# Head norm of an mLSTM block: quotient folded into the norm, squares and gating moved to earlier units

## The chip, the cores and the metric

The kernel runs on one core of a Trainium2 chip. The metric is the time of one execution in microseconds of the device. A core has TensorE (PE; PEld is its weight load), VectorE (DVE), ScalarE (ACT), GpSimd (POOL) and the DMA queues, here above all SyncE's (SP). Each engine runs its own list of instructions in order and waits on semaphores.

## The reference, cut to what matters

The program is a decoder trunk of two layers on 256 tokens of width 1024 in float32. Only the end of the mLSTM mixer of layer 0 is touched. Per head (4 heads, value width 256) the reference computes

```
h = num / jnp.maximum(jnp.abs(den), jnp.exp(-m_t))[..., None]
...
h = h * lax.rsqrt(jnp.mean(h * h, axis=-1, keepdims=True) + EPS) * hnorm_g
h = h.astype(x.dtype) * jax.nn.sigmoid(o.reshape(Bsz, S, A_HEADS, A_V_DIM))
return h.reshape(Bsz, S, nv) @ w_out
```

`o` is a projection of the same normed input as q, k and v; `w_out` is the output projection, followed by the residual and a gated ConvFFN. With d = max(|den|, exp(-m_t)) the first two lines equal num / sqrt(mean(num^2) + EPS d^2), times the gain.

## The kernel before, in words

Every weight is cut into units of 1024 rows by 256 columns. Unit n lies in slot n % 3 of a ring: SP loads it into `raw` (`load`, L359; for n >= 3 it waits until the slot's low parts are done), ScalarE rounds it to a high part `whi` (`hi`, L505, which waits for the load and for TensorE's last use of the slot), and the low part `wlo = raw - whi` is computed in two halves (`lo`) by VectorE for slots 0 and 1 (L852) and by GpSimd for slot 2 (L464, four instructions). TensorE multiplies a unit as two column tiles (c 0 and 1), for each of 8 row blocks k with three matmuls (high by high, high by low, low by high): 48 matmuls (`unit`, L1319), the second half of the rows only when the second half of `wlo` is there. `part` runs some k only; with `k_wait` a unit goes k by k instead of tile by tile.

Units 0 to 11 are the input projection: 0 to 3 are q and k, 4 to 7 are v, 8 to 11 are o. Units 12 to 15 are the output projection (`U_AOUT` is 12), 16 onwards the first FFN. The order on each engine is written out by hand: each has a loop over u, and what lies between the units' own steps is placed by u and c. Behind unit u TensorE puts: u 5 the scores; u 6, 7 and 8 the denominators (matmuls with ones, into bank 7) and numerators (bank 3 + h) of heads 0 and 1, of head 2, of head 3; u 7 and u 9 the column sums of the squares `hsq` of heads 0 and 1 and of heads 2 and 3 (into banks 3 and 4).

VectorE reads each tile of a unit out of PSUM; ahead of the tile (u, c) it puts `head_done(h)` (L957: maximum with `EB`, reciprocal, product into `hm`) at (7,0), (7,1), (8,0), (9,0), and `head_normed(h)` (L971: reciprocal of `hroot`, product on `hm`) at (8,1), (9,1), (10,0), (10,1). At u 11, before the two tiles, `gated` (L897: `hm` times gain times sigmoid) and then `m_lo` (L905: the low part of the activation into `xsB`) run for k 0 to 3, and after the loop for 4 to 7. `lo(u + 2)` stands first in each u.

ScalarE has at u 7 to 9 `Abs` of the denominators and `Square` of `hm`; at u 8 and 10 the square root; `gate` (L550, the sigmoid of a tile) for k 0 to 3 at u 10; `m_hi` (L555) for k 0 to 3 at u 11, later ones and `hi(14)` after the loop. `hi(u + 3)` ends each u but the last.

TensorE's `outproj` (L1471) runs unit 12 for k 0 to 5 (`HEAD_K` is 6), waiting for `m_lo` of each k, then waits for VectorE's last tile, runs unit 13 for k 0 to 5, then k 6 and 7 of both, then units 14 and 15. The same function runs layer 1's output projection (`begun` is true there). VectorE's `outproj` (L1077) adds the residual and makes the FFN's input (`gained`, L880) and the sum of its squares; the FFN's norm and the first taps (`cb`, L1107 and L1111) follow.

Of the kernel before, what the change touches and what calls it, by code (L numbers as in the profile page):

```python
# [16 lines left out]
P = 128  # L17
D = 1024
S = 256
# [74 lines left out]
def build(nc, xT, vectors, b_if, a_w_in, a_w_out, w_kv, b_w_q, b_w_out, rel_bias, f_w_up,  # L94
          f_w_down, onehot, mask, group, out):
    ctx = ExitStack()
    with ctx:
# [115 lines left out]
        def sq(q):  # L213
# [40 lines left out]
        den_done, den_abs, dmax_done, dinv_done = (sem("den_done"), sem("den_abs"),  # L254
                                                   sem("dmax_done"), sem("dinv_done"))
        num_done, hm_done, hsq_done = sem("num_done"), sem("hm_done"), sem("hsq_done")
# [245 lines left out]
        def _(act):  # L502
# [96 lines left out]
            for u in range(12):  # L599
# [17 lines left out]
                if u == 5:  # L617

                    for b in range(2):
                        act.wait_ge(eb_done, b + 1)  # L620
                        a.activation(EB[:, 2 * b:2 * b + 2, :],
                                     bank[(3, 7)[b]][:, :].rearrange("p (h t) -> p h t", h=2),
                                     ACT.Copy).then_inc(eb_copied, 1)
                    for e in range(2 * AH):
# [4 lines left out]
                            .then_inc(dm_exp, 1)  # L629
                for h in {7: (0, 1), 8: (2,), 9: (3,)}.get(u, ()):  # L630

                    act.wait_ge(den_done, max(h + 1, 2))
                    a.activation(den[:, h, :], bank[7][:, (h % 2) * S:(h % 2 + 1) * S], ACT.Abs)\
                        .then_inc(den_abs, 1)
                    act.wait_ge(hm_done, h + 1)
                    a.activation(hsq[:, h, :, :], hm[:, h, :, :], ACT.Square).then_inc(hsq_done, 1)
                if u in (8, 10):
                    b = u // 10
                    act.wait_ge(hss_done, b + 1)
                    a.activation(hroot[:, 2 * b:2 * b + 2, :],  # L640
                                 bank[3 + b][:, :].rearrange("p (h t) -> p h t", h=2),
                                 ACT.Sqrt, bias=epsc[:, 0:1], scale=1.0 / DV)\
                        .then_inc(hroot_done, 1)
# [12 lines left out]
            for k in range(4, KD):  # L656
                m_hi(k)
            hi(14)

# [189 lines left out]
        def _(dve):  # L849
# [107 lines left out]
            def head_done(h):  # L957

                dve.wait_ge(den_abs, h + 1)
                v.tensor_tensor(den[:, h, :], den[:, h, :], EB[:, h, :], ALU.max)\  # L960
                    .then_inc(dmax_done, 1)
                dve.wait_ge(dmax_done, h + 1)
                v.reciprocal(den[:, h, :], den[:, h, :]).then_inc(dinv_done, 1)
                dve.wait_ge(dinv_done, h + 1)
                dve.wait_ge(num_done, h + 1)
                v.tensor_tensor(hm[:, h, :, :],
                                bank[3 + h][:, :].rearrange("p (c t) -> p c t", c=2),
                                den[:, h:h + 1, :].to_broadcast([P, 2, S]), ALU.mult)\
                    .then_inc(hm_done, 1)

            def head_normed(h):  # L971
# [4 lines left out]
                v.tensor_tensor(hm[:, h, :, :], hm[:, h, :, :],  # L976
# [3 lines left out]
            for u in range(12):  # L980
                lo(u + 2)
# [65 lines left out]
                if u == 11:  # L1047
                    for k in range(4):
                        gated(k)
                    for k in range(4):  # L1050
                        m_lo(k)
                for c in range(2):

                    if (u, c) in ((7, 0), (7, 1), (8, 0), (9, 0)):
                        head_done(((7, 0), (7, 1), (8, 0), (9, 0)).index((u, c)))
                    if (u, c) in ((8, 1), (9, 1), (10, 0), (10, 1)):
# [652 lines left out]
```

## Time and profile before

| | |
|---|---|
| median of 3 runs | 792.14 us (792.02 to 792.15) |
| the profiled execution | 791.78 us, its span 789.7 us |
| busy share PE / DVE / ACT / POOL | 97% / 68% / 58% / 29% |
| mean granted clock | 0.993 |
| the part touched | about 62 to 118 us of the span |

A row of a timeline gives start, duration, engine, line, operation and tiles; xN merges N instructions, and the brackets show the idle time before it and who ended it. Successive instructions of an engine overlap a little in the records, so a step is read as the distance of two starts. The PSUM tensor of banks 3 to 5 and that of 6 and 7 are both shown as `banks`.

### The profile page before, as it was taken

How to read it: one execution, taken by the hardware profiler on the slowest of the kernel's cores; microseconds unless marked ns; L12 is line 12 of the kernel's file. 1: busy time of each engine (PE TensorE's matmuls, PEld its weight loads, DVE VectorE, ACT ScalarE, POOL GpSimd, SP SyncE). 2: the span in 40 equal slices, each digit the busy share in tenths (PEclk: the TensorE clock that was granted, in tenths of full speed). 3: DMA queues.
4: the chain of work that ended last, by engine and by line, in shares of the span. 5: the costliest groups of instructions: out<-in, count | busy, mean ns of one | idle time of the engine just before them, and what ended most of it. 6: DMA issues, size and time to landing. Idle time of an engine off the chain costs nothing.

```text
span 789.7 us, 17137 instructions
## 1 busy us (share of the span) xinstructions
PE 765.8 (97%) x6534; PEld 751.4 (95%) x6534; DVE 535.2 (68%) x983; ACT 458.6 (58%) x608; POOL 226.7 (29%) x190
## 2 busy tenths in 40 slices
PE   8999989999999999999999999999999999999995
PEld 8989889999999999999999999999998999999995
DVE  5776867888878744646646646565678888788442
ACT  6552546756566546447647746835856665665451
POOL 2520222523422342222222220311232234222331
PEclk9999999999999999999999999999999999999998
DMA  9653426565555566754473374474426655554721
GB/s 293 203 165 107 135 82 212 174 200 190 182 182 184 186 193 205 226 191 141 131 236 128 104 246 149 149 230 139 152 83 201 226 186 187 183 189 147 238 93 53
DMA packets 139804, 136.23 MB, mean 173 GB/s; under 512 B 3585, under 2 KB 139089, under 8 KB 139764
## 3 DMA queue, kind: packets, MB, share of 16 engines
q1 hardware_dynamic: 127968, 130.11, 50.9%
q10 hardware_dynamic: 11796, 5.56, 2.8%
q8 instruction: 27, 0.44, 0.2%
q14 instruction: 13, 0.11, 0.1%
HBM read 134.54 MB, written 1.13 MB: 172 GB/s over the span
## 4 chain that ended last, share of the span: by engine, by line
PE 57%; DVE 22%; issue 10%; ACT 7%; DVEq 1%; DMA 1%; ACTq 0%; POOL 0%; POOLq 0%
DVE wlo L860 8%; PE bank L1315 7%; PE bank L1317 7%; PE bank L1316 7%; PE banks L1315 6%; PE banks L1317 6%; PE banks L1316 6%; PE bank L1539 3%; DVE cb L1107 3%; PE bank L1541 3%; PE bank L1540 3%; PE banks L1601 2%; ACT cb L690 2%; DVE bank L1101 2%; PE banks L1573 2%
## 5 line engine op out<-in xcount | busy, mean ns | idle before, releaser
L471 POOL TENSOR_TENSOR wlo<-raw,whi 128x512 fp32r<-128x512 f32 (+1 forms) x169 | 218.1, 1322 | 526.5 <-ACT whi L512 526.5
L512 ACT ACTIVATE whi<-raw 128x2048 fp32r<-128x2048 f32 (+1 forms) x136 | 238.1, 1751 | 199.2 <-PE bank L1317 106.1
L860 DVE TENSOR_TENSOR wlo<-raw,whi 128x1024 fp32r<-128x1024 f32 x161 | 197.1, 1262 | 15.0 <-ACT whi L512 14.3
L1315 PE MATMUL bank<-xsA,whi 128*128 128x256 f32 x568 | 159.4, 281 | 2.9 <-DVE wlo L937 1.9
L1317 PE MATMUL bank<-xsA,wlo 128*128 128x256 f32 x568 | 157.7, 278 | 0.0
L1316 PE MATMUL bank<-xsA,whi 128*128 128x256 f32 x568 | 157.6, 278 | 0.0
L1315 PE MATMUL bank<-xsB,whi 128*128 128x256 f32 x480 | 134.0, 279 | 0.4 <-DVE cb L1111 0.3
L1317 PE MATMUL bank<-xsB,wlo 128*128 128x256 f32 x480 | 132.6, 276 | 0.0
L1316 PE MATMUL bank<-xsB,whi 128*128 128x256 f32 x480 | 132.6, 276 | 0.0
L1315 PEld LDWEIGHTS bank<-xsA,whi 128*128 128x128 f32 x568 | 107.5, 189 | 4.7 <-issue 3.7
L1316 PEld LDWEIGHTS bank<-xsA,whi 128*128 128x128 f32 x568 | 107.5, 189 | 0.1
L1317 PEld LDWEIGHTS bank<-xsA,wlo 128*128 128x128 f32 x568 | 107.4, 189 | 0.0
L1315 PE MATMUL banks<-hs,whi 128*128 128x256 f32 x352 | 97.2, 276 | 0.0
L1316 PE MATMUL banks<-hs,whi 128*128 128x256 f32 x352 | 97.2, 276 | 0.0
L1317 PE MATMUL banks<-hs,wlo 128*128 128x256 f32 x352 | 97.2, 276 | 0.0
L1315 PEld LDWEIGHTS bank<-xsB,whi 128*128 128x128 f32 x480 | 90.1, 188 | 1.4 <-DVE cb L1111 0.5
L1316 PEld LDWEIGHTS bank<-xsB,whi 128*128 128x128 f32 x480 | 90.2, 188 | 0.0
L1317 PEld LDWEIGHTS bank<-xsB,wlo 128*128 128x128 f32 x480 | 90.1, 188 | 0.0
L1315 PEld LDWEIGHTS banks<-hs,whi 128*128 128x128 f32 x352 | 66.1, 188 | 0.0
L1317 PEld LDWEIGHTS banks<-hs,wlo 128*128 128x128 f32 x352 | 66.1, 188 | 0.0
L1316 PEld LDWEIGHTS banks<-hs,whi 128*128 128x128 f32 x352 | 66.1, 188 | 0.0
L1539 PE MATMUL bank<-whi,xsA 128*128 128x256 f32 x192 | 56.7, 296 | 0.0
(200 smaller groups left out, 1572.3 us busy)
## 6 DMA issues: line engine op xcount, KB each, us to landing
raw<-in_f_w_up SPq DMA_DIRECT2D x44, 1024.0 KB, 5.1
raw<-in_w_kv SPq DMA_DIRECT2D x24, 1024.0 KB, 5.3
raw<-in_f_w_down SPq DMA_DIRECT2D x16, 1024.0 KB, 5.1
raw<-in_b_w_q SPq DMA_DIRECT2D x12, 1024.0 KB, 5.3
raw<-in_a_w_in SPq DMA_DIRECT2D x10, 1024.0 KB, 5.8
raw<-in_f_w_down SPq DMA_DIRECT2D x8, 768.0 KB, 4.9
Bi<-bias_by_distance ACTq DMA_DIRECT2D x16, 320.0 KB, 4.6
raw<-in_a_w_out SPq DMA_DIRECT2D x4, 1024.0 KB, 5.2
```

The source lines that it names most:

```text
L471: o = g.tensor_tensor(wlo[s][:, ka:kb, :], raw[s][:, ka * CW:kb * CW] .rearrange("p (k c) -> p k c", c=CW), whi[s][:, ka:kb, :].bitcast(F3 ...
L512: o = a.activation(whi[s][:, k0:k1, :], raw[s][:, k0 * CW:k1 * CW] .rearrange("p (k c) -> p k c", c=CW), ACT.Copy)
L690: a.activation(cb[:, j, :], bank[FB[j]][:, 0:S], ACT.Identity, scale=conv_col(layer, 2, ch), bias=conv_col(layer, 3, ch))\
L860: v.tensor_tensor(wlo[s][:, ka:kb, :], raw[s][:, ka * CW:kb * CW].rearrange("p (k c) -> p k c", c=CW), whi[s][:, ka:kb, :].bitcast(F32), A ...
L1101: v.tensor_tensor(u, u, rstd[:, 0:S], ALU.mult).then_inc(ev_done, 1)
L1107: v.scalar_tensor_tensor(cb[:, j, 1:S], bank[FB[j]][:, 0:S - 1], conv_col(layer, 1, p * 2 + (KF * g + c)), cb[:, j, 1:S], ALU.mult, ALU.ad ...
L1315: t_.matmul(ps, hi_w, hi_x, start=first, stop=False)
L1316: t_.matmul(ps, hi_w, lo_x, start=False, stop=False)
L1317: return t_.matmul(ps, lo_w, hi_x, start=False, stop=last)
L1539: t_.matmul(ps, xs[:, k, 0, cs], whi[s][:, k, :], start=first, stop=False)
L1540: t_.matmul(ps, xs[:, k, 0, cs], wlo[s][:, k, :], start=False, stop=False)
L1541: mm = t_.matmul(ps, xs[:, k, 1, cs], whi[s][:, k, :], start=False, stop=last)
```

## The change

The denominators and `exp(-m)` are squared as they leave PSUM (`EB`, `den`), their maximum is taken for two heads at once (`den_bounded`), and `Square` reads the numerators from PSUM. `squares_joined` forms sum/(DV EPS) + d^2 for two heads; the root with scale EPS gives `hroot`, and `head_normed` multiplies the numerator in PSUM by its reciprocal. `head_done` and its reciprocals are gone.

On TensorE all four denominators follow unit 6 (banks 7 and 6). The squares of heads 0 and 1 are summed behind unit 7, those of heads 2 and 3 between k 3 and k 4 of unit 9, which now runs k 0 to 3 of both tiles first. Layer 0's output projection is cut at k 4 in place of 6. `gate` for k 0 to 3 moves to u 9 on ScalarE (before `hi(12)`), `m_hi` for them to u 10 (before `hi(13)`), `hi(14)` ahead of `m_hi(6)`. On VectorE `gated` 0 to 3 moves to (10,0), `lo(12)` to (11,0), and `lo(13)` behind the loop, one half after `gated` 4 and 5, the other after `gated` 6 and 7.

```diff
@@ ScalarE
-                                     ACT.Copy).then_inc(eb_copied, 1)
+                                     ACT.Square).then_inc(eb_copied, 1)
...
+                if u == 7:
+                    for b in range(2):
+                        act.wait_ge(den_done, 2 * b + 2)
+                        a.activation(den[:, 2 * b:2 * b + 2, :],
+                                     bank[7 - b][:, :].rearrange("p (h t) -> p h t", h=2),
+                                     ACT.Square).then_inc(den_sq, 1)
                 for h in {7: (0, 1), 8: (2,), 9: (3,)}.get(u, ()):
-                    act.wait_ge(den_done, max(h + 1, 2))
-                    a.activation(den[:, h, :], bank[7][:, (h % 2) * S:(h % 2 + 1) * S], ACT.Abs)\
-                        .then_inc(den_abs, 1)
-                    act.wait_ge(hm_done, h + 1)
-                    a.activation(hsq[:, h, :, :], hm[:, h, :, :], ACT.Square).then_inc(hsq_done, 1)
-                if u in (8, 10):
...
+                    act.wait_ge(num_done, h + 1)
+                    a.activation(hsq[:, h, :, :],
+                                 bank[3 + h][:, :].rearrange("p (c t) -> p c t", c=2), ACT.Square)\
+                        .then_inc(hsq_done, 1)
+                if u in (8, 9):
+                    b = u - 8
+                    act.wait_ge(hsum_done, 2 * b + 2)
+                    a.activation(hroot[:, 2 * b:2 * b + 2, :], hroot[:, 2 * b:2 * b + 2, :],
+                                 ACT.Sqrt, scale=EPS).then_inc(hroot_done, 1)
+                if u == 9:
+                    for k in range(4):
+                        gate(k)
                 if u == 10:
                     for k in range(4):
-                        gate(k)
+                        m_hi(k)
                 if u == 11:
                     for k in (4, 5):
                         gate(k)
-                    for k in range(4):
-                        m_hi(k)
                 else:
                     hi(u + 3)
             for k in (6, 7):
                 gate(k)
-            for k in range(4, KD):
+            for k in (4, 5):
                 m_hi(k)
             hi(14)
+            for k in (6, 7):
+                m_hi(k)
@@ VectorE
+            def den_bounded(b):
+                dve.wait_ge(den_sq, b + 1)
+                v.tensor_tensor(den[:, pair(b), :], den[:, pair(b), :], EB[:, pair(b), :], ALU.max)\
+                    .then_inc(dmax_done, 1)
+            def squares_joined(b):
+                dve.wait_ge(dmax_done, b + 1)
+                dve.wait_ge(hss_done, b + 1)
+                v.scalar_tensor_tensor(hroot[:, pair(b), :],
+                                       bank[7][:, :].rearrange("p (h t) -> p h t", h=2),
+                                       1.0 / (DV * EPS), den[:, pair(b), :], ALU.mult, ALU.add)\
+                    .then_inc(hsum_done, 2)
             def head_normed(h):
...
-                v.tensor_tensor(hm[:, h, :, :], hm[:, h, :, :],
+                v.tensor_tensor(hm[:, h, :, :],
+                                bank[3 + h][:, :].rearrange("p (c t) -> p c t", c=2),
                                 hrs[:, h:h + 1, :].to_broadcast([P, 2, S]), ALU.mult)\
                     .then_inc(hn_done, 1)
             for u in range(12):
-                lo(u + 2)
+                if u < 10:
+                    lo(u + 2)
...
+                    if (u, c) in ((7, 1), (9, 0)):
+                        den_bounded((u - 7) // 2)
+                    if (u, c) in ((8, 0), (9, 1)):
+                        squares_joined(u - 8)
+                    if (u, c) in ((8, 1), (9, 0), (10, 0), (10, 1)):
+                        head_normed(((8, 1), (9, 0), (10, 0), (10, 1)).index((u, c)))
+                    if (u, c) == (10, 0):
+                        for k in range(4):
+                            gated(k)
+                    if (u, c) == (11, 0):
+                        lo(U_AOUT)
+                        for k in range(4):
+                            m_lo(k)
...
             for k in (4, 6):
                 gated(k)
                 gated(k + 1)
+                lo(U_AOUT + 1, k0=KD // 2 * (k // 6), k1=KD // 2 * (k // 6 + 1))
                 m_lo(k)
                 m_lo(k + 1)
@@ TensorE
+                if u == 9:
+                    unit(U_IN + 9, xsA, [in_bank(18), in_bank(19)], wait_bank=waits, part=(0, 4))
+                    pe.wait_ge(hsum_done, 2)
+                    squares(1)
...
+                for h in range(AH) if u == 6 else ():
+                    pe.wait_ge(sd_done, h + 1 if h < 2 else AH)
+                    ps = bank[7 - h // 2][:, (h % 2) * S:(h % 2 + 1) * S]
...
+                if u == 7:
+                    pe.wait_ge(den_sq, 1)
+                    squares(0)
...
-                unit(u0 + 1, xs, banks[1], part=(0, HEAD_K))
-                unit(u0, xs, banks[0], k_wait=k_wait, part=(HEAD_K, KD))
-                unit(u0 + 1, xs, banks[1], part=(HEAD_K, KD))
+                unit(u0 + 1, xs, banks[1], part=(0, k0))
+                unit(u0, xs, banks[0], k_wait=k_wait, part=(k0, KD))
+                unit(u0 + 1, xs, banks[1], part=(k0, KD))
```

Here `k0` is 6 when `begun`, else 4; `squares(b)` waits for `hsq_done` of each head and sums the squares of two heads into bank 7.

## Rows read from the trace of the kernel before

**Rows 1.** The page: busy time of TensorE; a kind of weight load, KB, us to landing.

```profile
PE 765.8 (97%) x6534; PEld 751.4 (95%) x6534; DVE 535.2 (68%) x983; ACT 458.6 (58%) x608; POOL 226.7 (29%) x190
...
raw<-in_f_w_up SPq DMA_DIRECT2D x44, 1024.0 KB, 5.1
```

**Rows 2.** TensorE's waits, whole span: us in total, times, longest.

```profile
PE banks L1315 <- DVE cb L1111: 3.2, 7, 1.3
PE banks L1315 <- DVE xsB L908: 2.3, 1, 2.3
...
PE banks L1466 <- ACT hsq L636: 1.7, 1, 1.7
...
PE bank L1315 <- DVE X L927: 0.7, 1, 0.7
```

**Rows 3.** Timeline of TensorE: starts of units 9, 10, 12, 14, squares, end of 11.

```profile
82.83 0.36 PE L1315 MATMUL bank<-xsA,whi 128*128 128x256 f32 x1
...
88.40 0.59 PE L1466 MATMUL banks<-hsq,ones 128*128 128x256 f32 x2
...
91.08 0.70 PE L1466 MATMUL banks<-hsq,ones 128*128 128x256 f32 x2 [1.66 <-ACT hsq L636]
...
91.86 0.47 PE L1315 MATMUL bank<-xsA,whi 128*128 128x256 f32 x1
...
102.84 0.28 PE L1317 MATMUL bank<-xsA,wlo 128*128 128x256 f32 x1
105.47 0.36 PE L1315 MATMUL banks<-xsB,whi 128*128 128x256 f32 x1 [2.35 <-DVE xsB L908]
...
118.07 0.28 PE L1315 MATMUL bank<-xsB,whi 128*128 128x256 f32 x1
```

**Rows 4.** A window behind unit 12's start: busy by engine, clock, DMA share, GB/s.

```profile
106.10:109.40 3.30, 3.30 (x17) 3.30 (x17) 3.21 (x9) 1.82 (x5) 0.00 (x0) 0.50 0.56 194
```

**Rows 5.** A group of VectorE, 60 to 111: count, busy us, mean ns, idle before.

```profile
L963 DVE RECIPROCAL den<-den 128x256 f32<-128x256 f32 x4 | 7.0, 1753 | 0.1
```

**Rows 6.** Timeline of VectorE, 98 to 106.

```profile
98.33 1.74 DVE L974 RECIPROCAL hrs<-hroot 128x256 f32<-128x256 f32 x1
100.11 0.69 DVE L976 TENSOR_TENSOR hm<-hm,hrs 128x512 f32<-128x512 f32 x1
100.72 0.42 DVE L1069 TENSOR_TENSOR sig<-bank,rstd 128x256 f32<-128x256 f32 x1
101.05 2.35 DVE L860 TENSOR_TENSOR wlo<-raw,whi 128x1024 fp32r<-128x1024 f32 x2
103.32 1.67 DVE L902 SCALAR_TENSOR_TENSOR hm<-hm,vcols,sig 128x256 f32<-128x256 f32 x4
104.90 1.43 DVE L908 TENSOR_TENSOR xsB<-hm,xsB 128x256 fp32r<-128x256 f32 x4
```

**Rows 7.** Timeline of ScalarE, 92 to 97.

```profile
92.74 0.67 ACT L640 ACTIVATE hroot<-banks,epsc 128x512 f32<-128x512 f32 x1
93.43 1.28 ACT L553 ACT_TABLE_LOAD   x1
94.72 1.34 ACT L553 ACTIVATE sig<-sig 128x256 f32<-128x256 f32 x4
```

**Rows 8.** VectorE's and GpSimd's `lo` side by side, layer 1; GpSimd's alone.

```profile
588.38 3.56 DVE L860 TENSOR_TENSOR wlo<-raw,whi 128x1024 fp32r<-128x1024 f32 x2
...
584.43 6.42 POOL L471 TENSOR_TENSOR wlo<-raw,whi 128x512 fp32r<-128x512 f32 x4 [23.41 <-ACT whi L512]
...
111.82 5.04 POOL L471 TENSOR_TENSOR wlo<-raw,whi 128x512 fp32r<-128x512 f32 x4 [20.36 <-ACT whi L512]
```

**Rows 9.** ScalarE at layer 0's FFN norm; VectorE's last residuals in layer 1.

```profile
136.01 1.90 ACT L512 ACTIVATE whi<-raw 128x2048 fp32r<-128x2048 f32 x1
137.81 0.45 ACT L547 ACTIVATE rstd<-banks,epsc 128x256 f32<-128x256 f32 x1
...
597.70 0.73 DVE L927 TENSOR_TENSOR X<-X,bank 128x256 f32<-128x256 f32 x2
```

More of the change, by code:

```diff
@@ L1046, in _ @@
                             .then_inc(sd_done, 1)
[L1047 to L1051, printed above, removed]
-                for c in range(2):
-                    if (u, c) in ((7, 0), (7, 1), (8, 0), (9, 0)):
-                        head_done(((7, 0), (7, 1), (8, 0), (9, 0)).index((u, c)))
-                    if (u, c) in ((8, 1), (9, 1), (10, 0), (10, 1)):
-                        head_normed(((8, 1), (9, 1), (10, 0), (10, 1)).index((u, c)))
+                for c in range(2):
+                    if (u, c) in ((7, 1), (9, 0)):
[11 more added lines that the diff above has]
+                            m_lo(k)
                     t = 2 * u + c
@@ L1377, in first_wait, with squares @@
                     pe.wait_ge(lo_done[0], 2)
+            def squares(b):
+                for h in (2 * b, 2 * b + 1):
+                    pe.wait_ge(hsq_done, h + 1)
+                    ps = bank[7][:, (h % 2) * S:(h % 2 + 1) * S]
+                    t_.matmul(ps, ones[:], hsq[:, h, 0, :], start=True, stop=False)
+                    mm = t_.matmul(ps, ones[:], hsq[:, h, 1, :], start=False, stop=True)
+                mm.then_inc(hss_done, 1)
             pe.wait_ge(consts, 2)
@@ L1453, in _ @@
                     pe.wait_ge(ev_done, 2 * (4 + h) + 2)
+                    if h == 3:
+                        pe.wait_ge(den_sq, 2)
                     for c in range(2):
@@ L1460, in _ @@
                     mm.then_inc(num_done, 1)
-                if u in (7, 9):
-                    for h in (0, 1) if u == 7 else (2, 3):
-                        pe.wait_ge(hsq_done, h + 1)
-                        ps = bank[3 + h // 2][:, (h % 2) * S:(h % 2 + 1) * S]
-                        t_.matmul(ps, ones[:], hsq[:, h, 0, :], start=True, stop=False)
-                        mm = t_.matmul(ps, ones[:], hsq[:, h, 1, :], start=False, stop=True)
-                        if h % 2:
-                            mm.then_inc(hss_done, 1)
+                if u == 7:
+                    pe.wait_ge(den_sq, 1)
+                    squares(0)
             def outproj(u0, e0, xs, k_wait, q0, banks, begun):
+                k0 = HEAD_K if begun else KD // 2
                 if not begun:
-                    unit(u0, xs, banks[0], k_wait=k_wait, part=(0, HEAD_K))
+                    unit(u0, xs, banks[0], k_wait=k_wait, part=(0, k0))
                 pe.wait_ge(ev_done, e0)
```

32 lines of the change are left out of this document (6 added, 26 removed).

## The prediction, made before the changed kernel ran

> **What bounds the kernel now.** I read the page first: TensorE is busy 97% of the span [rows 1], so only time in which it waits, or runs slowly, is to be had. Then its waits over the whole span [rows 2]: the largest single ones are 2.3 us on `xsB` (L908) and 1.7 us on `hsq` (L636), both inside the change, and 1.3 and 0.7 us on `cb` and `X`, just behind it. The timeline of TensorE places them [rows 3]. Unit 9 begins at 82.83, the squares of heads 2 and 3 at 88.40; head 3's pair runs from 91.08 to 91.86 (0.8 a head), so it was due at 89.2 and is 1.8 late. Units 10 and 11 end with the matmul of 102.84. Unit 12 begins at 105.47 instead of 102.95: 2.5 lost. Unit 14, behind the change, begins at 118.07. A window shows one loss more [rows 4]: from 106.1 to 109.4, behind that idle time, the granted clock is 0.50 (1.2 GHz, not 2.4), and 3.3 us at half rate lose 1.65. From unit 9 to unit 14, then, 1.8 + 2.5 + 1.65 = 5.95 us are lost. The cause is VectorE, which from 95 to 106 goes from one instruction to the next [rows 6] while ScalarE waits for it.
>
> **The change, part by part.** (1) The quotient goes. VectorE loses four reciprocals of 1.75 us (7.0) [rows 5], and four products of `hm` like the one at 100.11 (0.69 each, 2.8) [rows 6]; four maxima of 128x256 become two of 128x512, by the rows of these two sizes (0.42 and 0.69) 0.3 less in all. It gains two `squares_joined` of 128x512 from PSUM. The trace has no such form; bounds are 0.42 (a 128x256 read of PSUM, row 100.72) and 1.75 (a reciprocal); I take 0.7, the 128x512 row at 100.11. Net about 8.7 us less on VectorE (7.0 + 2.8 + 0.3 - 1.4). ScalarE trades four `Abs` for two `Square` of twice the width: nothing. More important: `hsq` no longer waits for VectorE. ScalarE can square head 3 as soon as its numerator is in PSUM and `hi(11)` is through, about 84.2.
>
> (2) TensorE's work does not change in amount. The denominators of heads 2 and 3 move from behind units 7 and 8 into the group behind unit 6, so unit 8 begins 0.7 later and unit 9 at the same 82.83. Half of unit 9 (24 matmuls, 2.85) ends at 85.7; squares until 87.2, with no wait since 84.2 is before 85.7; unit 10 begins near 90.1 (before 91.86). The split restarts the pipeline once more, 0.2. At (102.84 - 91.86) for 95 matmuls, unit 11 ends at 101.2.
>
> (3) The new VectorE chain. Steps are distances of starts in [rows 6]: a product 0.61, a tile read 0.33, a `lo` of two 2.27 (half 1.13), four `gated` 1.58 (0.395 each), four `m_lo` 1.35 (0.34 each); a reciprocal and its hand-over 1.78. Reading (9,0) now comes at three quarters of unit 9, 89.0. Then `squares_joined(1)` 89.3 to 90.0; `hroot` on ScalarE 0.67 [rows 7], 90.8; `head_normed(2)` to 93.2; `gated` 0 to 3 to 94.8 (their sigmoids: table load 1.28 and 0.33 each [rows 7], first at 92.4, last at 93.4, never late); tile, `head_normed(3)`, tile: 97.8; `lo(12)` to 100.1; `m_lo` 0 to 3 from 100.1 to 101.5, the first before unit 11 ends. So unit 12 starts without a wait at 101.2, and with no idle time ahead of it I expect clock 1.00. Its first half lasts to 104.0. VectorE meanwhile: two tiles 102.1, `gated` 4 and 5 102.9, first half of `lo(13)` 104.1. New wait: 0.2. `m_lo` 4, 5 to 104.7, `gated` 6, 7 to 105.5.
>
> The Trainium skill (ScalarE: Activation LUTs, What ACT_TABLE_LOAD costs) gives a table load 1.28 us plus a drain of 1.38. The row agrees on the load and not on the drain: the sigmoid starts at 94.72, 0.01 after the load of 93.43 ends [rows 7]. By the page the first `gated` would come 0.6 later and the gain be 0.6 less; the measurement decides.
>
> (4) What is late next. `hi(14)` now stands before `m_hi(6)`, at about 103.4 to 105.3 (before 109.84), so GpSimd's `lo(14)` starts at 105.3, beside VectorE's `gated(7)`, `lo(13)` second half, `m_lo(6)` and `m_lo(7)`. Such a meeting shows in [rows 8]: two halves of `lo` that take 2.35 alone took 3.56, and GpSimd's four took 6.42 (5.04 in other places, 1.26 each): they alternate, and a VectorE instruction with two SBUF inputs waits for a whole GpSimd one, 1.2. With three such waits: `lo(13)` ends 107.9, `m_lo(6)` 109.4, `m_lo(7)` 111.0. TensorE ends the first half of unit 13 at 107.0 and wants k 6 at 108.4: waits of 1.1 and 0.8. The bounds are 0 (VectorE wins each time) and 3.0 (another turn lost). The Trainium skill (SBUF — State Buffer, Who interferes with whom) says the one that issues first gets the shared ports for the whole instruction, which would make the order at 105.3 decide; with VectorE first at each turn the sum would lose nothing here.
>
> Sum to unit 14: 5.95 - 0.2 (split) - 0.2 - 1.9 = 3.65; it begins at 114.4.
>
> (5) Behind it. SP's loads of 15 and 16 are issued when `lo(12)` and `lo(13)` are done, 100.1 and 107.9, that is 4.5 later than now, and land 5.1 later [rows 1], 105.2 and 113.0. ScalarE wants them at about 111.9 and 115.1: hidden, by 2 at the least. The load of 17 is earlier. Unit 12 now ends 2.8 before unit 14 begins (1.4 before), so `hi(15)`, the residuals, `lo(15)` and `lo(16)` are about 1.5 earlier against TensorE, and two `gained` no longer meet GpSimd. The 0.7 wait for `X` [rows 2] and its restart go: 0.9. The next is the root of the FFN norm: it runs at 137.81, held by a weight copy of 1.9 before it [rows 9], though the sums were issued near 136.0, so it is 1.4 late. In layer 1 the same holds (597.70 [rows 9]: the last residuals wait there for a `lo` on VectorE); in layer 0 that `lo` is GpSimd's, so they can move up. I expect the root 1.2 earlier against TensorE and `lo(19)` clear of GpSimd, and the waits for `cb` (1.3 and a short one, with restarts 1.8) to shrink by 1.6. From there each pair is TensorE's. Total 3.65 + 0.9 + 1.6 = 6.2. The profiled execution took 791.78 (span 789.7 and 2.1 around it) and would take 785.6; the median of the runs, 792.14, is 0.36 above it: **785.9**.
>
> **The rivals.** *VectorE is not held by GpSimd*: the 1.9 does not arise, gain 8.1, 784.0. For it: the semaphores may fall so that `lo(13)` is issued before GpSimd's first; against it [rows 8]. *The gain behind unit 14 is not had*: 3.65 alone, 788.5. For it: layer 1 has no wait for `X` and still waits on `cb`; against it the place of that `lo`. *The wait moves into unit 9 or 10*: if `squares_joined`, `hroot` and `gated` come 1 later than worked out, unit 12's first half pays it: gain 5.2, 786.9. *Slower*: the waits of 0.2, 1.1 and 0.8 come within 10 us, and the clock falls as it did at 106.1 [rows 4] but stays at 0.50 for the rest of the output projection. From the first fall at 108 to the end near 125, 17 us of which half is loss: 8.5 against the 6.2, 794.4. It decides from about 12 us at half clock. For it: the clock did fall here; against it: it fell behind 2.4 idle us and not behind the 1.7 at 91 or the 1.3 in the FFN [rows 2]. *The change does not do what it says*: the mean square of the unnormed numerator plus EPS times the squared denominator is the same norm, and no step waits for its own result, so I give it nothing.
>
> **Chances.** Forecast 50%, no hold 17%, nothing behind 15%, chain late 12%, slower 4%, 2% between. Something under 0.2% (1.6 us, about what can't be told from no change) needs most of the forecast to fail. Range 783.8 to 788.6: the first and second rival lie just inside. Faster 0.94, same 0.02, slower 0.04.
>
> **What would show it.** In the profile after: `hsq` reads a bank and TensorE has no wait for it; unit 12 at about 101 without a wait and clock 1.00 through 100 to 125; waits of TensorE on `xsB` L908's counterpart of about 2 us in sum, with VectorE's `lo(13)` and `m_lo` longer than 1.22 and 0.42; unit 14 near 114.4; no wait for `X`; the wait of 1.3 for `cb` nearly gone. The prediction is wrong if TensorE waits in unit 9, if the clock falls, or if what is gained at unit 14 is not at least kept at the end.

## The result, and the profile after

The changed kernel takes 783.12 us (782.97 to 783.64, 4 runs) and the kernel before 792.14 on the same chip; the ratio of the two is 0.989, 95% interval 0.9876 to 0.9905. The prediction was 785.9 with a range of 783.8 to 788.6: the sign was right, the gain was 9.0 us and not 6.2, and the time lies 0.7 below the range. The profiled execution has a span of 781.1 us, 8.6 less than before.

TensorE's waits over the whole span, in the profile after (us in total, times, longest); the rows for `hsq`, `xsB` and `X` of [rows 2] are gone, and one wait for `wlo` is new:

```profile
PE banks L1332 <- DVE cb L1128: 2.2, 7, 1.2
...
PE bank L1332 <- DVE wlo L865: 0.3, 1, 0.3
```

The timeline of TensorE in the profile after answers to [rows 3]: start of unit 9, squares of heads 2 and 3 in its middle, start of unit 12, of unit 13 with its wait, of unit 14, of unit 16 (first FFN unit):

```profile
83.22 0.36 PE L1332 MATMUL bank<-xsA,whi 128*128 128x256 f32 x1
...
86.07 0.38 PE L1403 MATMUL banks<-hsq,ones 128*128 128x256 f32 x1
...
101.42 0.28 PE L1332 MATMUL banks<-xsB,whi 128*128 128x256 f32 x1
...
104.56 0.35 PE L1332 MATMUL bank<-xsB,whi 128*128 128x256 f32 x1 [0.26 <-DVE wlo L865]
...
112.81 0.28 PE L1332 MATMUL bank<-xsB,whi 128*128 128x256 f32 x1
...
123.69 0.28 PE L1332 MATMUL bank<-xsA,whi 128*128 128x256 f32 x1
```

Unit 9 begins 0.39 us later than before. That comes from the prologue, where nothing was edited, so I count from unit 9. Unit 14 comes 29.59 us behind it (35.24 before): 5.65 gained, where 3.65 was forecast. Unit 16 comes 40.47 behind it; it began at 129.81 before, 46.98 behind: 6.5 gained in all. Unit 19, the second unit of the FFN's second pair, begins at 140.88, and at 149.40 before: 8.9 gained. From there on the two traces run alike, and less the 0.39 this is the 8.6 of the spans to 0.1.

The windows after (columns as in [rows 4]) have the clock at 1.00 from unit 12 on, where the kernel before had 0.50:

```profile
101.40:104.40 3.00, 2.90 (x26) 2.70 (x24) 3.00 (x8) 2.21 (x5) 0.00 (x0) 1.00 0.88 294
104.40:110.00 5.60, 5.44 (x48) 5.47 (x49) 3.56 (x9) 1.93 (x3) 4.39 (x2) 1.00 0.39 124
```

VectorE's timeline after, where [rows 6] had its packed stretch; the chain is the one that the prediction wrote down, and ends 0.3 us behind it (the prologue's 0.39):

```profile
89.72 0.68 DVE L976 SCALAR_TENSOR_TENSOR hroot<-banks,den 128x512 f32<-128x512 f32 x1
...
91.10 1.75 DVE L984 RECIPROCAL hrs<-hroot 128x256 f32<-128x256 f32 x1
92.89 0.69 DVE L986 TENSOR_TENSOR hm<-banks,hrs 128x512 f32<-128x512 f32 x1
93.50 1.66 DVE L907 SCALAR_TENSOR_TENSOR hm<-hm,vcols,sig 128x256 f32<-128x256 f32 x4
...
98.13 2.35 DVE L865 TENSOR_TENSOR wlo<-raw,whi 128x1024 fp32r<-128x1024 f32 x2
100.40 1.42 DVE L913 TENSOR_TENSOR xsB<-hm,xsB 128x256 fp32r<-128x256 f32 x4
```

What was misjudged shows where GpSimd's `lo(14)` meets VectorE. First VectorE, then GpSimd, each instruction by itself:

```profile
105.40 0.48 DVE L907 SCALAR_TENSOR_TENSOR hm<-hm,vcols,sig 128x256 f32<-128x256 f32 x1
105.80 1.22 DVE L865 TENSOR_TENSOR wlo<-raw,whi 128x1024 fp32r<-128x1024 f32 x1
106.93 0.42 DVE L913 TENSOR_TENSOR xsB<-hm,xsB 128x256 fp32r<-128x256 f32 x1
107.27 0.42 DVE L913 TENSOR_TENSOR xsB<-hm,xsB 128x256 fp32r<-128x256 f32 x1
...
105.61 3.23 POOL L470 TENSOR_TENSOR wlo<-raw,whi 128x512 fp32r<-128x512 f32 x1 [16.36 <-ACT whi L511]
108.80 1.29 POOL L470 TENSOR_TENSOR wlo<-raw,whi 128x512 fp32r<-128x512 f32 x1
```

VectorE's four instructions keep their lengths. GpSimd's first one takes 3.23 us, not 1.29: it waits until VectorE's last `m_lo` ends at 107.69. The prediction had it the other way round.

### The profile page after: what moved, and what is told of

The parts are those of the page before. It is cut to its first block, busy times and chain, and to the rows that moved or that the text cites. A ratio compares the mean times of both kernels' runs of the same rounds, so it can differ in the third digit from the quotient of the medians.

```text
span 781.1 us, 17126 instructions
## 1 busy us (share of the span) xinstructions
PE 762.8 (98%) x6534; PEld 749.3 (96%) x6534; DVE 525.0 (67%) x975; ACT 457.9 (59%) x606; POOL 226.9 (29%) x190
## 4 chain that ended last, share of the span: by engine, by line
PE 62%; DVE 19%; issue 10%; ACT 5%; DMA 1%; DVEq 1%; ACTq 0%; POOL 0%; POOLq 0%
PE bank L1332 8%; PE bank L1333 8%; PE bank L1334 8%; DVE wlo L865 6%; PE banks L1332 6%; PE banks L1333 6%; PE banks L1334 6%; DVE cb L1124 3%; PE bank L1564 3%; PE bank L1566 3%; PE bank L1565 3%; PE banks L1626 2%; DVE bank L1118 2%; ACT cb L695 2%; PE banks L1598 2%
```

## The experiments

Medians of 4 to 12 runs. A ratio is a kernel's time to that of the kernel before, run beside it. "Against 783.1" means the changed kernel, which ran again (`after_again`) on the chip of `e_mid`, `e_cut6` and `e_gate11`; the other kernels ran on other chips, so differences of less than 1 us from it are not told apart there by the times alone. Gains and losses at a unit are counted from the start of unit 9.

> The changed kernel once more, beside its variants on the same chip. All theories: 783.1 us, 9.0 under the kernel before.

Measured 783.05 (782.83 to 783.61), ratio 0.9899 (0.9881 to 0.9916).

**GpSimd let in 2 us earlier.** `hi(14)` ahead of the gates of k 6 and 7 (`e_pool`):

```diff
                 if u == 11:
                     for k in (4, 5):
                         gate(k)
-                else:
-                    hi(u + 3)
+                hi(u + 3)
             for k in (6, 7):
                 gate(k)
-            for k in (4, 5):
-                m_hi(k)
-            hi(14)
-            for k in (6, 7):
+            for k in (4, 5, 6, 7):
                 m_hi(k)
```

> The changed kernel with hi(14) ahead of the gates of k 6 and 7, so that GpSimd's lo(14) asks for the ports at about 103.5, 2 us earlier, while VectorE is in the first half of lo(13), and VectorE then has a gap before m_lo(4). Theory A, that GpSimd gets in only where VectorE leaves a gap between instructions with two SBUF inputs: here it gets in, m_lo 4 to 7 and lo(13) wait one to three GpSimd instructions, and TensorE waits 1 to 2.5 us: 784.1 to 785.6. Theory B, that VectorE always wins: 783.1 to 783.4.

Measured 786.93, ratio 0.9947 (0.993 to 0.9964): 3.9 against 783.1, more than either theory had. VectorE's instructions from 104 on, then GpSimd's first ones, in the trace of this kernel:

```profile
104.20 1.28 DVE L909 TENSOR_TENSOR xsB<-hm,xsB 128x256 fp32r<-128x256 f32 x1
105.41 1.51 DVE L909 TENSOR_TENSOR xsB<-hm,xsB 128x256 fp32r<-128x256 f32 x1
106.84 1.51 DVE L903 SCALAR_TENSOR_TENSOR hm<-hm,vcols,sig 128x256 f32<-128x256 f32 x1
108.28 1.49 DVE L903 SCALAR_TENSOR_TENSOR hm<-hm,vcols,sig 128x256 f32<-128x256 f32 x1
...
103.33 1.88 POOL L470 TENSOR_TENSOR wlo<-raw,whi 128x512 fp32r<-128x512 f32 x1 [14.43 <-ACT whi L511]
105.16 1.48 POOL L470 TENSOR_TENSOR wlo<-raw,whi 128x512 fp32r<-128x512 f32 x1
```

VectorE's first half of `lo(13)` ends at 104.07 and `m_lo(4)` starts at 104.20. There GpSimd, which has asked since 103.33, gets in, and from then on each VectorE instruction waits for one of GpSimd's: four that take 0.42 or 0.48 alone take 1.28 to 1.51, 4.0 us more in sum. TensorE then waits for `m_lo(6)`, which stands behind these four and the second half of `lo(13)` and comes at 110.8:

```profile
PE banks L1328 <- DVE xsB L909: 2.7, 1, 2.7
```

and behind this idle time the granted clock is 0.50 again (from 112.5 to 115.7; the matmuls come 0.21 apart). Theory B falls: VectorE is held by GpSimd, and here that costs 3.9 us, about 1.6 of them by the half clock, where in the changed kernel the same meeting 2 us later costs nothing. Two things differ, the instant of the request and the pause of 0.13 us; the runs below take them apart.

**The opposite.** `hi(14)` behind `m_hi` 6 and 7 (`hi14_last`):

```diff
-            for k in (4, 5):
-                m_hi(k)
-            hi(14)
-            for k in (6, 7):
+            for k in range(4, KD):
                 m_hi(k)
+            hi(14)
```

> The changed kernel with hi(14) behind m_hi 6 and 7 again, so that GpSimd's lo(14) asks for the ports at about 106.5. Theory A, from the trace of the changed kernel, that the meeting at 105.6 costs VectorE nothing: 783.1. Theory of the prediction, that it costs 1 to 2 us wherever it happens: it is shorter here, 782 to 782.7.

Measured 784.33 (783.46 to 784.34), ratio 0.9909 (0.9892 to 0.9927), against 783.1: slower by 1.2 in the medians, which neither theory had; but two of the five runs, at 783.46 and 783.65, lie where the changed kernel's upper ones do, and the two intervals overlap. GpSimd asks at 108.19, behind VectorE's last `m_lo` (107.66), so there is no meeting at all, and at unit 14 it is where the changed kernel is: the meeting at 105.6 was indeed free. The loss lies behind (1.0 us by unit 19 in this trace, of a run at 784.33): `lo(14)` ends at 113.2 instead of 112.6, SP's load of unit 17 waits for it, ScalarE waits for that load (its `hi(17)`: first the changed kernel's, then this one's), and `lo(17)` meets one `gained` more:

```profile
118.79 1.92 ACT L511 ACTIVATE whi<-raw 128x2048 fp32r<-128x2048 f32 x1 [1.92 <-DMA raw<-in_f_w_up]
```

```profile
119.88 1.92 ACT L511 ACTIVATE whi<-raw 128x2048 fp32r<-128x2048 f32 x1 [3.05 <-DMA raw<-in_f_w_up]
...
122.30 1.16 DVE L883 SCALAR_TENSOR_TENSOR xsA<-X,vcols,xsA 128x256 fp32r<-128x256 f32 x1 [0.40 <-ACT xsA L522]
...
PE banks L1330 <- DVE cb L1126: 1.1, 1, 1.1
```

**The last wait taken away.** First half of `lo(13)` ahead of `gated` 4 and 5 (`e_lo13`):

```diff
             for k in (4, 6):
+                if k == 4:
+                    lo(U_AOUT + 1, k1=KD // 2)
                 gated(k)
                 gated(k + 1)
-                lo(U_AOUT + 1, k0=KD // 2 * (k // 6), k1=KD // 2 * (k // 6 + 1))
+                if k == 6:
+                    lo(U_AOUT + 1, k0=KD // 2)
```

> The changed kernel with the first half of lo(13) ahead of gated 4 and 5 instead of behind them. Theory: TensorE's last wait here (0.3 us, restart 0.2, at 104.56) goes and nothing else is late: 782.6 to 782.8. Rival, that VectorE then leaves a gap before m_lo(4) or lets GpSimd in at 105.6: 783.5 to 785.

Measured 784.84 (784.72 to 785.24), ratio 0.9921 (0.9906 to 0.9936), against 783.1. The rival holds. The wait before unit 13 is gone, but the last `m_lo` pair now meets GpSimd, 2.93 us where it took 0.76, and TensorE waits 0.8 for it in two pieces and, behind unit 18, 1.0 more for `cb`. At unit 14 the loss is 0.86, at unit 19 it is 1.78:

```profile
107.21 2.93 DVE L913 TENSOR_TENSOR xsB<-hm,xsB 128x256 fp32r<-128x256 f32 x2
...
106.79 1.64 POOL L470 TENSOR_TENSOR wlo<-raw,whi 128x512 fp32r<-128x512 f32 x1 [17.49 <-ACT whi L511]
```

VectorE leaves no gap here: the second half of `lo(13)` runs from 106.07 to 107.28, `m_lo(6)` starts at 107.21. GpSimd asked 0.72 after that half began, and got in when it ended.

**Only the request moved.** `n` copies on ScalarE, 0.33 us each, ahead of `hi(14)` in the changed kernel (`ask1`, `ask2`, `ask3` with n = 1, 2, 3):

```diff
                 m_hi(k)
+            for i in range(n):
+                a.activation(hsq[:, i, 0, :], hsq[:, i, 1, :], ACT.Copy)
             hi(14)
```

> The changed kernel with one ScalarE copy of 128x256 (0.33 us, its result read by nobody) ahead of hi(14), so that GpSimd asks for lo(14) at about 105.9 and not at 105.61: at the start of the long second half of lo(13) (105.80 to 107.02), and no longer during gated(7). Nothing else moves that TensorE waits for. Theory 'gap': VectorE's three instructions follow each other directly, so GpSimd waits until 107.69 as before, m_lo 6 and 7 take 0.42 each, and the time is 783.0 to 783.5. Theory 'early request': GpSimd's request, standing well before the end of the second half of lo(13), is taken at its end as in the kernel with lo(13) early; m_lo 6 and 7 wait about 1.1 us each, TensorE waits for them and for cb, 784.3 to 785.2.

> The same with two copies: GpSimd asks at about 106.27, 0.75 before the second half of lo(13) ends. Theory 'gap': 783.0 to 783.6, GpSimd's first instruction ends after 107.69 + 1.2 with VectorE's m_lo at 0.42 each. Theory 'early request': 784.3 to 785.2, m_lo pair about 2.9 us in place of 0.76.

> The same with three copies: GpSimd asks at about 106.6, 0.42 before the second half of lo(13) ends, the distance (0.49) at which it got in in the kernel with lo(13) early. m_hi(6) now ends at about 106.9, at the very start of m_lo(6), so a gap of up to 0.1 us may open for it. Theory 'gap': no meeting cost if none opens, 783.2 to 783.8. Theory 'early request': as with two copies, 784.3 to 785.2. If the first two are free and this one isn't, it is the gap of m_lo(6) that lets GpSimd in.

Measured 783.46 (783.34 to 783.48), 783.33 (782.75 to 784.01) and 783.04 (782.8 to 784.58), with ratios of 0.9909, 0.9906 and 0.9902 (intervals of 0.002 each way). "Early request" falls: up to unit 14 the three traces are the changed kernel's within 0.03 us. GpSimd asked at 105.95, 106.30 and 106.54, and each time it waited until VectorE's last `m_lo` was done. With three copies, where the distances are those of `e_lo13` (0.74 behind the start of the half of `lo(13)`):

```profile
105.80 1.22 DVE L867 TENSOR_TENSOR wlo<-raw,whi 128x1024 fp32r<-128x1024 f32 x1
106.93 0.75 DVE L915 TENSOR_TENSOR xsB<-hm,xsB 128x256 fp32r<-128x256 f32 x2
...
106.54 2.30 POOL L470 TENSOR_TENSOR wlo<-raw,whi 128x512 fp32r<-128x512 f32 x1 [17.28 <-ACT whi L511]
```

The profiled execution of `ask3` is the one at 784.58, the highest of its four. It loses its 1.1 us elsewhere, at a second meeting, of GpSimd's `lo(17)` with VectorE's `gained` for column 4; behind it TensorE waits 1.26 us for `cb` (at 139.16). The same two instructions, first in the changed kernel's trace, then in that of `ask3`:

```profile
120.79 1.29 POOL L470 TENSOR_TENSOR wlo<-raw,whi 128x512 fp32r<-128x512 f32 x1 [8.17 <-ACT whi L511]
121.95 0.48 DVE L885 SCALAR_TENSOR_TENSOR xsA<-X,vcols,xsA 128x256 fp32r<-128x256 f32 x1 [0.32 <-ACT xsA L522]
```

```profile
120.74 1.29 POOL L470 TENSOR_TENSOR wlo<-raw,whi 128x512 fp32r<-128x512 f32 x1 [8.14 <-ACT whi L511]
121.95 1.62 DVE L887 SCALAR_TENSOR_TENSOR xsA<-X,vcols,xsA 128x256 fp32r<-128x256 f32 x1 [0.31 <-ACT xsA L522]
```

VectorE asks at the same 121.95. GpSimd's first instruction ends at 122.08 in the one and VectorE goes next; it ends at 122.03 in the other, and GpSimd's second goes first. In nine traces VectorE asked 0.13 to 0.89 us before that end and always went next (0.48 to 1.16 us); in `e_lo13`, `lo13_d1`, `lo13_d2` and `b_cut4` (below) it asked 0.12 to 0.14 behind it and waited for the whole next one (1.40 to 1.42). In the first three this goes with the part of their loss that lies behind unit 14, 0.9 to 1.0. So at this meeting the instant goes with the outcome, and a shift of 0.05 us goes with 1.1 us of time. No run moved it on purpose.

**Only VectorE moved, in the other order.** `n` memsets of 0.27 us on VectorE in `e_lo13` (`lo13_d1`, `lo13_d2` with n = 1, 2):

```diff
                     lo(U_AOUT + 1, k1=KD // 2)
+                if k == 6:
+                    for i in range(n):
+                        v.memset(hsq[:, i, 0, :], 0.0)
                 gated(k)
```

> The kernel with the first half of lo(13) early, and one VectorE memset of 128x256 (0.27 us) ahead of gated(6), so that VectorE's second half of lo(13) starts 0.27 later while GpSimd's request stays at 106.79: 0.45 after its start and no longer 0.72. Theory 'instant': what let GpSimd in there was the instant of the request within VectorE's instruction; m_lo 6 and 7 now take 0.42 each, and the time is 783.2 to 783.9, up to 1.5 faster than without the memset although VectorE does more. Theory 'context': something else of that order lets it in (the instant was excluded by ask3, which had the same 0.74); the m_lo pair takes about 2.9 again and the time is 784.8 to 785.4.

> The same with two memsets (0.54 us), the request 0.18 after the start of VectorE's second half of lo(13). Theory 'instant': m_lo pair 0.76 us, 783.3 to 784.1. Theory 'context': m_lo pair 2.9, 785.0 to 785.7.

Measured 784.82 (ratio 0.9924, 0.9901 to 0.9947) and 785.13 (0.9929, 0.9906 to 0.9952): as `e_lo13`. "Instant" falls for the meeting with `lo(14)`. With two memsets the request stands 0.30 behind the start of the half of `lo(13)`, which begins at 106.19, and GpSimd gets in at its end all the same:

```profile
107.33 2.92 DVE L913 TENSOR_TENSOR xsB<-hm,xsB 128x256 fp32r<-128x256 f32 x2
...
106.49 2.06 POOL L470 TENSOR_TENSOR wlo<-raw,whi 128x512 fp32r<-128x512 f32 x1 [17.50 <-ACT whi L511]
```

**Only a gap made** (`gap`). All kernels that lose have a pause of about 0.1 us in VectorE's stream near the meeting (in `e_lo13` at 104.45, where `m_lo(4)` waits for ScalarE), and of those that lose nothing none has one after 98:

```diff
             for k in (4, 6):
+                if k == 4:
+                    dve.wait_ge(sig_done, 7)
                 gated(k)
```

> The changed kernel with one wait added on VectorE, ahead of gated(4): for ScalarE's sig(6), which ends at about 102.6 where VectorE is free at 102.48. Order and instructions stay as they are; VectorE only gets one gap of about 0.15 us, 3 us before GpSimd's request at 105.61. Theory 'gap since': GpSimd is held off as long as VectorE's stream has had no gap since about 98 (so in every kernel that lost nothing), and once VectorE has paused, however early, GpSimd gets in behind the instruction that runs when it asks (so in the two kernels with lo(13) early and their variants, with a gap of 0.09 at 104.4, and in the one with GpSimd 2 us earlier, 0.13): VectorE's lo(13) second half or the m_lo pair takes 1.1 or 2.2 us longer and the time is 784.5 to 786.5. Theory 'order': the gap is of no account and it is something else of the order with lo(13) early; the instructions keep their lengths, everything on VectorE comes 0.15 later and the time is 783.1 to 783.6.

Measured 783.18 (782.96 to 783.33), ratio 0.9898 (0.9878 to 0.9917). The pause is there and lets nobody in; unit 14 is 0.24 us later, since TensorE's wait for `wlo` grows from 0.26 to 0.49:

```profile
102.31 0.88 DVE L907 SCALAR_TENSOR_TENSOR hm<-hm,vcols,sig 128x256 f32<-128x256 f32 x2 [0.15 <-ACT sig L552]
...
106.84 0.76 DVE L913 TENSOR_TENSOR xsB<-hm,xsB 128x256 fp32r<-128x256 f32 x2
```

"Gap since" falls too. So at this meeting neither the instant within the long instruction nor an earlier pause, each by itself, decides who goes first; the order with `lo(13)` ahead of `gated(4)` brings the loss each time, in four kernels, and the changed kernel's order never does, with the request at 105.5 to 106.5, in five. Three further kernels with this end of the order, `e_cut6`, `e_gate11` and `e_mid` (requests at 105.31, 105.33 and 106.66), lose nothing at it either. What of the other order does it was not found. One rival is untested: in the four kernels VectorE's pause, ahead of `m_lo(4)`, ends 2.25 us before the request, in `gap` 3.2 us before it and ahead of another instruction.

**Cut at k 6** (`e_cut6`) on the changed kernel, and **cut at k 4** (`b_cut4`) on the kernel before:

```diff
-                k0 = HEAD_K if begun else KD // 2
+                k0 = HEAD_K
```

> The changed kernel with layer 0's output projection cut at k 6 as before, not at k 4. Theory, that the gain behind unit 14 (3.3 us more at unit 19 than at unit 14) comes from unit 12 ending 2.8 and not 1.4 us before unit 14 begins: half to all of it is lost, 784.8 to 786.4. Rival, that it comes from GpSimd and ScalarE being free earlier whatever the cut: 783.1 to 783.5.

> The kernel before with one edit: layer 0's output projection cut at k 4 instead of k 6. Theory, that an earlier end of unit 12 against unit 14 gives what was gained behind unit 14: the wait for X (0.7) goes and the root of the FFN norm is earlier, 789 to 790.5 for 792.1. Rival, that the cut is worth nothing by itself: 792.1; it may also cost, since unit 13 then needs lo(13) no later than before and k 4 and 5 later, not more than 0.3.

Measured 786.64 (786.46 to 786.85), 3.6 against 783.1 and just above the forecast, and 788.16 for 791.63 (ratio 0.9963, 0.9947 to 0.9979), 3.5 less in the medians, more than forecast. By the ratio it is 2.9 less (1.7 to 4.2), and by the two profiled executions, which both have the half clock behind the wait for `xsB`, 2.7. Of the parts tested one by one the cut is the largest. With the cut at 6 the loss is nearly all behind unit 14 (unit 14 starts 0.35 later against unit 9, unit 19 3.6 later), and the old waits are back:

```profile
PE banks L1332 <- DVE cb L1128: 1.3, 1, 1.3
PE bank L1332 <- DVE X L932: 0.7, 1, 0.7
```

VectorE's `gained` for columns 2 and 3, first with the cut at 6, then in the changed kernel, show one cause: in the first they fall beside GpSimd's `lo(17)`, which starts at 120.55; in the second they are through before it starts at 120.79.

```profile
120.83 1.53 DVE L885 SCALAR_TENSOR_TENSOR xsA<-X,vcols,xsA 128x256 fp32r<-128x256 f32 x1
...
122.62 1.18 DVE L885 SCALAR_TENSOR_TENSOR xsA<-X,vcols,xsA 128x256 fp32r<-128x256 f32 x1
```

```profile
119.43 0.48 DVE L885 SCALAR_TENSOR_TENSOR xsA<-X,vcols,xsA 128x256 fp32r<-128x256 f32 x1
...
120.16 0.48 DVE L885 SCALAR_TENSOR_TENSOR xsA<-X,vcols,xsA 128x256 fp32r<-128x256 f32 x1
```

**GpSimd taken away from them instead** (`c6_hi17`: cut at 6, `hi(17)` one unit later):

```diff
-                    for n in ((4,), (5,), (), (6,))[u]:
+                    for n in (((4,), (), (5,), (6,)) if u0 == U_AOUT else ((4,), (5,), (), (6,)))[u]:
```

> The kernel cut at k 6 (786.6 us) with one more edit: in layer 0's output projection ScalarE's hi(17) stands behind the high parts of columns 4 and 5 instead of behind those of 2 and 3, so that GpSimd's lo(17) starts some 4 us later. Theory, that the cut at k 4 gains 3.5 us because VectorE's gained(2) and (3) then run before lo(17) and don't wait for GpSimd (0.48 us each, not 1.53 and 1.18): most of the wait for X goes here too, and the FFN's root comes earlier, 784.5 to 785.8. Rival, that what counts is the 1.4 us by which unit 12 ends earlier: 786.4 to 786.8. Rival, that lo(17) only hits later instructions: 786.6 or more.

Measured 785.35 (785.05 to 785.72), ratio 0.9927 (0.9912 to 0.9942): 1.3 of the 3.6 back without the cut. The wait for `X` is gone; `lo(17)`, from 126.28, now hits `gained` 6 and 7 (waits of 0.5 for `xsA`, 0.7 for `cb`). So about a third of the cut's gain comes back by moving GpSimd's meeting with `gained` alone, and the moved meeting has its own price; whether the rest is the earlier end of unit 12 was not shown.

**Both local edits** (`best`: `e_lo13` and the late `hi(17)` on the changed kernel):

> The changed kernel with both edits: first half of lo(13) ahead of gated 4 and 5, and hi(17) behind columns 4 and 5. Theory: the first gives 0.4, the second spares gained(5) and (6) the 0.7 and 0.9 that they wait for GpSimd and takes the rest of the wait for cb (0.3): 782.0 to 782.7. Rival, that lo(18) and lo(17) then run back to back into the FFN's first lo and taps: 783 to 784.

Measured 784.73, ratio 0.9918 (0.9902 to 0.9933), 2 us above the forecast and above the rival too. Unit 14's side loses the same as in `e_lo13` (`m_lo` pair 2.94). Neither edit helps; none of my kernels beats the changed one.

**Squares behind unit 9** (`e_mid`; the block of unit 9 in the loop goes, and `squares(1)` follows the unit):

```diff
-                if u == 9:
-                    unit(U_IN + 9, xsA, [in_bank(18), in_bank(19)], wait_bank=waits, part=(0, 4))
-                    pe.wait_ge(hsum_done, 2)
-                    squares(1)
```

> The changed kernel with the squares of heads 2 and 3 summed behind unit 9 instead of in its middle. Theory of the VectorE chain: squares_joined(1) starts about 0.7 us later (90.4 for 89.7), everything to lo(13) follows, TensorE's wait before unit 13 grows from 0.3 to about 1.0 and one restart of 0.2 goes: 783.6 to 783.9. Rival, that the removed wait of 1.7 on hsq comes back here: 784.8. Rival, that the place in unit 9 is worth nothing: 783.1.

Measured 784.82 (784.35 to 785.48), ratio 0.9921 (0.9903 to 0.9939): 1.8 against 783.1, where I had 0.5 to 0.8. `squares_joined(1)` starts at 90.76 for 89.72, 1.04 later and not 0.7, and TensorE waits twice, for `xsB` (0.5) and for `wlo` (0.6): 1.1 at unit 14, the rest behind it. The number is that of the rival with the wait for `hsq`, but not its cause: the trace has no wait for `hsq`. Unit 9 with its squares takes 7.11 us here and 7.32 in the changed kernel, so the split costs the 0.2 that the prediction took for it.

**Gating in unit 11 again** (`e_gate11`; `gate`, `gated` and `m_hi` of k 0 to 3 one unit later, `gated` behind `lo(12)`):

```diff
-                if u == 9:
-                    for k in range(4):
-                        gate(k)
                 if u == 10:
                     for k in range(4):
-                        m_hi(k)
+                        gate(k)
...
-                    if (u, c) == (10, 0):
+                    if (u, c) == (11, 0):
+                        lo(U_AOUT)
                         for k in range(4):
                             gated(k)
-                    if (u, c) == (11, 0):
-                        lo(U_AOUT)
```

> The changed kernel with k 0 to 3 gated in unit 11 again (gate at u 10, gated behind lo(12), m_hi after that), the rest unchanged. Theory, that VectorE's chain is bound by its sum and not by its order: the 1.6 us of gated only move behind lo(12), first m_lo at the same 100.4: 783.1 to 783.5. Rival, that gating in unit 10 is what lets ScalarE's high parts be ready: m_lo waits for m_hi and hi(13), hi(14) come later, 784 to 785.5.

Measured 783.17 (782.89 to 784.47), ratio 0.9904 (0.9886 to 0.9922): no difference. On VectorE `m_lo` starts at 100.11 in place of 100.40, but unit 9 also begins 0.29 earlier, so it is the same place. This half of the change, named in its title, is worth nothing that these runs show.

**The arithmetic alone** (`e_math`, the old order with the new arithmetic):

> The changed arithmetic in the old order: quotient gone, Square from PSUM, denominators behind unit 6, but squares of heads 2 and 3 behind unit 9, root and gates of k 0 to 3 in unit 10, gated and m_lo of k 0 to 3 ahead of unit 11's tiles, lo(13) at unit 11, hi(14) last, cut at k 6. Theory, that the order gives most of the gain: the hsq wait goes (1.8) but unit 12 still waits for m_lo, about 3 us, and the clock falls: 789.5 to 791. Rival, that the 8.7 us less work on VectorE alone give the gain: 784 to 785.

Measured 789.93 (788.34 to 790.91) for 791.63, ratio 0.9989 (0.9975 to 1.0002), not told apart from the kernel before; the rival of 784 to 785 is out. Its trace has the `hsq` wait gone and a longer one in its place:

```profile
PE banks L1325 <- DVE xsB L910: 2.9, 1, 2.9
```

**The clock by itself** (`b_fill`, on the kernel before):

```diff
                 if not begun:
+                    for _ in range(10):
+                        t_.matmul(bank[7][:, 0:P], ones[:], ones[:], start=True, stop=True)
                     unit(u0, xs, banks[0], k_wait=k_wait, part=(0, HEAD_K))
```

> The kernel before with ten more matmuls of ones (128 columns, into a bank nobody reads) between units 11 and 12, where TensorE stands idle for 2.35 us. Theory, that the half clock from 106.1 to 109.4 follows from that idle time: the clock stays at 1.00, unit 12 starts at the same 105.5, and 1.65 us come back: 790.5. Rival, that the fall has another cause: 792.1. If what is won is eaten by waits on m_lo (the last at 110.4), 791.4.

Measured 790.6 (790.09 to 790.74) for 791.63, ratio 0.9991 (0.9982 to 1.0001): by median and ratio inconclusive. But none of the 12 runs is above 790.74, where 14 of the 24 of the kernel before on the same chip lie from 791.57 to 792.2, and the trace agrees: with the idle time filled, the clock stays at 1.00 and 29 matmuls are issued in the 3.3 us in which the kernel before issues 17 [rows 4]; counted from unit 9, unit 14 comes 1.3 us earlier.

```profile
106.10:109.40 3.30, 3.29 (x29) 3.12 (x29) 3.21 (x10) 1.54 (x5) 0.00 (x0) 1.00 0.63 218
```

The kernel before itself varies more than the others, 788.3 to 792.5 in 67 runs on the later chips: 29 lie below 790.6 and 38 above 791.5. Its profiled execution, with the half clock, is of the second group. The mean granted clock points the same way, 0.995 to 0.997 in the first group and 0.991 to 0.995 in the second. But the medians of the groups are 2.3 us apart and the half clock explains 1.3 to 1.65 of that, and no execution of the first group was profiled, so this stays open. It also means that the 9.0 us hold about 2 us which the kernel before loses only in most of its runs.

Nor does the length of the idle time alone decide. At 10 us, ahead of unit 0, TensorE stands idle in every kernel, and the clock behind it is 0.50 in ten of the twenty traces (idle for 1.85 to 3.58 us) and 1.00 in the other ten (1.80 to 2.81). First the changed kernel, idle for 2.00 us, then `ask3`, idle for 2.81:

```profile
10.10:13.50 3.40, 3.40 (x16) 3.40 (x17) 3.23 (x7) 3.27 (x7) 0.00 (x0) 0.50 1.10 347
```

```profile
10.10:13.50 3.40, 3.40 (x29) 3.36 (x30) 3.22 (x7) 3.27 (x6) 0.00 (x0) 1.00 1.10 348
```

## Why the prediction was right or wrong, by its steps

The step that failed is (4), the three waits of VectorE for GpSimd that were to cost TensorE 1.1 and 0.8. They cost nothing: with 3.65 + 1.9 the sum at unit 14 is 5.55, and 5.65 was measured. That alone gives 784.0, just inside the range; the term for the FFN's start in step (5), 1.6 where 2.4 was measured, takes the time below it. I read the alternation out of [rows 8] as a rule for every meeting. It is the course of a meeting once GpSimd has a turn, as in [rows 8], where GpSimd was running when VectorE came; whether GpSimd gets the first turn is a second question, for which I had no row, and here it waits instead. The rival "VectorE is not held by GpSimd" (784.0, 17%) had the right outcome in this place, but not as a property of the engines: in `e_pool` and `e_lo13` VectorE is held in its `m_lo`, 2.7 and 2.9 us for a pair that takes 0.76, and at unit 14 the two are 4.7 (half clock included) and 0.86 us later. That VectorE isn't held with the request anywhere from 105.5 to 106.5 is shown (`ask1` to `ask3`, `gap`); why is open.

The opening counts 2.3 and 1.7 us as TensorE's largest single waits; one of 1.9 us for `wlo`, at 10.04 in the prologue, is larger than the second. It lies outside the change, so no term hangs on it. Part (1) was right in size (two `squares_joined` took 0.68, I took 0.7) but not in weight: alone it brings at most 2 us. Part (2) was right: no wait in unit 9, unit 12 at 101.42 (forecast 101.2 and the prologue's 0.39), without a wait and at clock 1.00; the three losses of 1.8, 2.5 and 1.65 are gone. In part (3) the wait before unit 13 was forecast at 0.2 and is 0.26; the 0.6 that a drain behind the table load would have taken is not there, the sigmoid follows the load at once (92.38 behind 91.09 + 1.28). The order of `gated`, which part (3) carried along as it stood, was without effect (`e_gate11`).

Part (5) was right in its mechanism and too small. The 0.9 for `X` came as 0.86. Of 1.6 for the FFN's start, 2.4 was measured: the waits for `cb` shrank to 0.2 us in this place, and the last two row blocks of unit 16, whose inputs were late before, are in time as well; this term I had left out. `e_cut6` shows that it hangs on the cut at k 4: without it 3.2 of the 3.3 us gained behind unit 14 are gone. On the kernel before the cut gives 2.7 to 3.5 us (`b_cut4`), nearly all behind unit 14 too. SP's later loads were hidden as said, except one: ScalarE waits 1.92 us for unit 17's load. The forecast called that load "earlier". It costs nothing here; with 1.1 us more of it, `hi14_last` loses 1.0 behind unit 14 in its trace.

The slower rival (clock at half for the rest of the projection) did not come about, with one wait of 0.26 in place of three. "Nothing behind unit 14" and "chain late" did not either.

## What to carry to other kernels

Where the streams of VectorE and GpSimd meet, price the meeting at both ends, here 0 and about 1 us for each VectorE instruction in it; a row from another place of the trace shows one of the two, and does not tell which will come about. An experiment that moves one of the streams tells more than the argument did. A reordering pays at its end as much as at its start: the cut of the output projection, which looks like a detail, gave about 3.5 of 9.0 us, nearly all of it behind unit 14, two units behind where it was made. And an order that puts work earlier without shortening the sum in front of the next consumer gives nothing.

## What the runs showed of the hardware that was not expected

GpSimd waited up to 2.1 us for four VectorE instructions in a row (105.61 to 107.69), not for one, though it had asked while the first was running, and in `ask1` to `ask3` for three, asked at 105.95, 106.30 and 106.54. In another order of VectorE's work (`e_lo13`, `best`, `lo13_d1`, `lo13_d2`) it got in behind the one that was running, with requests at 0.30 to 0.73 behind its start. Once it has had a turn there, the two alternate, and a 128x256 operation on VectorE takes 1.28 to 1.51 us in place of 0.42 to 0.48. At the meeting with `lo(17)` VectorE, asking 0.13 us or more before GpSimd's instruction ended, went next, and asking 0.08 us before the end or later it did not; the records of GpSimd are rough, so these bounds are of this case. TensorE's granted clock fell to 0.50 in the middle of the kernel behind idle times of 2.33 and 2.35 us (`b_cut4`, before), 2.93 (`e_math`) and 2.72 (`e_pool`), and not behind 1.7, 1.3 or 0.3; with the 2.35 us filled by matmuls nobody reads it did not fall. At 10 us it fell behind an idle time of 1.85 us (before) and not behind 2.81 (`ask3`), so the length of the idle time alone does not tell whether the clock falls.
